# The last step of a decoder layer's output: part of y = x + rstd * out is scaled on ScalarE and added onto a copy of x by accumulating DMAs

## The reference

```
h = rmsnorm(x, g_pre);  proj = h @ w_in
yA = mLSTM branch of proj;  yB = gated-MLP branch of proj
merged = sigmoid(ga) * (yA @ w_pa) + sigmoid(gb) * (yB @ w_pb)
out = merged @ w_out
y = x + out * rsqrt(mean(out * out) + EPS) * g_post
```

## Time and profile before

| | us |
|---|---|
| median of 3 runs (lowest to highest) | 1534.61 (1534.37 to 1535.24) |
| the profiled execution, its own time | 1535.78 |
| its span, first to last instruction | 1534.3 |
| PE busy in the span | 1503.8 |
| from the last scalar rstd (L1619 begins at 1523.09) to the span's end | 11.2 |

### The profile page before, as it was taken

The page is one execution under the profiler, slowest core; times in us unless marked ns, Lnnn a source line. Parts: engine busy times, 40 slices in busy tenths (PEclk is TensorE's granted clock), DMA queues, the critical chain, the costliest instruction groups (busy, mean ns, idle before and its releaser), DMA issues.

```text
span 1534.3 us, 30736 instructions
## 1 busy us (share of the span) xinstructions
PE 1503.8 (98%) x11341; PEld 1497.0 (98%) x11341; DVE 892.8 (58%) x1526; ACT 658.3 (43%) x928; POOL 93.7 (6%) x171
## 2 busy tenths in 40 slices
PE   6999999999999999999999999999999999999996
PEld 6999999999999999999999999999999999999996
DVE  6756565654444457666766666666666644444444
ACT  6433433333333334454545454545444433333442
POOL 4000000001000000101010101001010000000000
PEclk9999999999999999999999999999999999999998
DMA  7664655556555554564738383747474555555553
GB/s 214 213 165 138 177 153 172 154 173 220 164 164 164 164 155 143 167 218 136 243 112 266 112 264 115 257 122 253 126 242 136 189 161 168 160 169 184 169 153 135
DMA packets 233905, 268.03 MB, mean 175 GB/s; under 512 B 9136, under 2 KB 222712, under 8 KB 232880
## 3 DMA queue, kind: packets, MB, share of 16 engines
q1 hardware_dynamic: 221472, 226.36, 49.3%
q0 software_dynamic: 12400, 41.23, 7.7%
HBM read 244.48 MB, written 23.06 MB: 174 GB/s over the span
## 4 chain that ended last, share of the span: by engine, by line
PE 92%; issue 6%; POOL 1%; DVE 1%; ACT 0%; DVEq 0%; POOLq 0%; ACTq 0%
PE ps L394 27%; PE ps L395 27%; PE ps L396 27%; PE ps L561 2%; PE ps L549 2%; PE ps L573 1%; PE ps L693 1%; PE ps L620 1%; PE ps L518 1%; DVE otok L1484 0%; PE ps L423 0%; PE ps L658 0%; PE ps L403 0%; PE ps L684 0%; PE ps L630 0%
## 5 line engine op out<-in xcount | busy, mean ns | idle before, releaser
L988 DVE TENSOR_TENSOR wlo<-raw,whi 128x1024 fp32r<-128x1024 f32 x416 | 507.9, 1224 | 558.0 <-ACT whi L745 556.3
L394 PE MATMUL ps<-xh,whi 128*128 128x288 f32 x2560 | 766.3, 299 | 0.0
L745 ACT ACTIVATE whi<-raw 128x1024 fp32r<-128x1024 f32 x416 | 440.5, 1059 | 746.1 <-PE ps L396 730.1
L396 PE MATMUL ps<-xh,wlo 128*128 128x288 f32 x2560 | 754.9, 295 | 0.0
L395 PE MATMUL ps<-xl,whi 128*128 128x288 f32 x2560 | 754.5, 295 | 0.0
L394 PEld LDWEIGHTS ps<-xh,whi 128*128 128x128 f32 x2560 | 481.1, 188 | 0.3
L395 PEld LDWEIGHTS ps<-xl,whi 128*128 128x128 f32 x2560 | 481.0, 188 | 0.2
L396 PEld LDWEIGHTS ps<-xh,wlo 128*128 128x128 f32 x2560 | 480.7, 188 | 0.0
L394 PE MATMUL ps<-yh,whi 128*128 128x288 f32 x512 | 151.6, 296 | 0.0
L395 PE MATMUL ps<-yl,whi 128*128 128x288 f32 x512 | 151.2, 295 | 0.0
L396 PE MATMUL ps<-yh,wlo 128*128 128x288 f32 x512 | 151.1, 295 | 0.0
(11 more groups left out here) (319 smaller groups left out, 1182.2 us busy)
## 6 DMA issues: line engine op xcount, KB each, us to landing
raw<-in_w_in_dram SPq DMA_DIRECT2D x320, 512.0 KB, 3.7
raw<-in_w_pb_dram SPq DMA_DIRECT2D x32, 512.0 KB, 3.5
Cin<-in_state_mlstm_C_dram POOLq DMA_DIRECT2D x16, 1024.0 KB, 8.7
out_dram<-Cin POOLq DMA_DIRECT2D x16, 1024.0 KB, 6.2
raw<-in_w_pa_dram SPq DMA_DIRECT2D x32, 512.0 KB, 3.5
raw<-in_w_out_dram SPq DMA_DIRECT2D x32, 512.0 KB, 3.6
xt<-in_x_prompt_dram SPq DMA_DIRECT2D x2, 1024.0 KB, 6.0
out_dram<-cpo POOLq DMA_DIRECT2D x8, 256.0 KB, 2.4
```

Source lines behind the costliest of these rows:

```text
L394: nc.tensor.matmul(out, whi[:, c, kk, cols], mh_[:, k, :], start=(k == 0), stop=False)
L396: last = nc.tensor.matmul(out, wlo[:, c, kk, cols], mh_[:, k, :], start=False, stop=(k == KT - 1))
L745: nc.scalar.activation(whi[:, c], raw[:, c], ACT.Copy).then_inc(hi_ready, 1)
L988: nc.vector.tensor_tensor(wlo[:, c], raw[:, c], whi[:, c].bitcast(F32), ALU.subtract).then_inc(lo_ready, 1)
```

## The change

Two of the six parts leave `Y_PARTS`: columns 1024 to 2047 of block 1 (128 x 1024) and block 2 (32 x 2048). For these, SP copies x straight from the input in DRAM to the output in DRAM (two DMAs, semaphore `y_base`), in its queue behind the load of `xres` and ahead of the stores; the load of the sample rows into `xres` is gone. ACT multiplies the two parts of `otok` by `rstd`, in place, once `o_rstd` and `otok_ev` are there (semaphore `y_scaled`). POOL, behind its power, waits for both copies and then for each part and issues a DMA from `otok` to the output that adds to what stands there (semaphore `y_sum`). It waits for both. DVE and SP keep the other four parts, in their order.

```
 Y_PARTS = ([(P, 0, slice(c, c + D // 4)) for c in (0, D // 4)] + [(P, 0, slice(D // 2, D))]
-           + [(P, 1, slice(c, c + D // 2)) for c in (0, D // 2)] + [(S, 2, slice(0, D))])
+           + [(P, 1, slice(0, D // 2))])
...
         sp.dma_start(xres[:, 0:2, :], xp_v).then_inc(x_again, 16)
-        sp.dma_start(xres[0:S, 2, :], xs_v).then_inc(x_again, 16)
-        y_rows = (y_prompt[0, 0:P, :], y_prompt[0, P:TP, :], y_sample.rearrange("b t d -> (b t) d"))
+        sp.dma_start(y_prompt[0, P:TP, HALVES[1]], x_prompt[0, P:TP, HALVES[1]]).then_inc(y_base, 16)
+        sp.dma_start(y_sample.rearrange("b t d -> (b t) d"), xs_v).then_inc(y_base, 16)
+        y_rows = (y_prompt[0, 0:P, :], y_prompt[0, P:TP, :])
...
         squares(1, 7)
+        act.wait_ge(o_rstd, 1)
+        act.wait_ge(otok_ev, 8)
+        for n, t, cols in ((P, 1, HALVES[1]), (S, 2, slice(0, D))):
+            nc.scalar.activation(otok[0:n, t, cols], otok[0:n, t, cols], ACT.Identity,
+                                 scale=rstd[0:n, t:t + 1]).then_inc(y_scaled, 1)
...
         dve.wait_ge(otok_ev, 8)
-        dve.wait_ge(x_again, 32)
+        dve.wait_ge(x_again, 16)
...
         nc.gpsimd.tensor_tensor(rstd[:], stat[:], half[:], ALU.pow).then_inc(o_rstd, 1)
+        pool.wait_ge(y_base, 32)
+        pool.wait_ge(y_scaled, 1)
+        pool.dma_start(y_prompt[0, P:TP, HALVES[1]], otok[:, 1, HALVES[1]], accum_op=ALU.add).then_inc(y_sum, 16)
+        pool.wait_ge(y_scaled, 2)
+        pool.dma_start(y_sample.rearrange("b t d -> (b t) d"), otok[0:S, 2, :], accum_op=ALU.add
+                       ).then_inc(y_sum, 16)
+        pool.wait_ge(y_sum, 32)
```

More of the change, by code:

```diff
@@ L298, in build @@
     cst_out, cp_out, nn_out, cs_out = sem("cst_out"), sem("cp_out"), sem("nn_out"), [sem("cs_out0"), sem("cs_out1")]
+    y_base, y_scaled, y_sum = sem("y_base"), sem("y_scaled"), sem("y_sum")
     x_again, g_post_in, o_sq, osq_set, o_var, o_rstd, y_set, y_out = (sem(n) for n in (
```

## The result

| | us |
|---|---|
| changed kernel, median of 11 runs (lowest to highest) | 1538.61 (1537.89 to 1539.25) |
| kernel before, timed beside it, median of 11 runs | 1535.24 (1533.97 to 1535.65) |
| ratio, 95% interval | 1.0023 (1.0016 to 1.0031) |
| changed kernel, profiled execution: its own time, its span | 1538.25, 1536.8 |

The kernel became 0.23% slower, 3.4 to 3.5 us. The time was inside the stated range (1533.0 to 1540.0), but not where the forecast stood (+0.6, with a band of its own from 0 to +1.5), and the ratio's interval lies on both sides of the 0.2% that was set as a bound. That the range held it owes much to luck: the range reached up to 1540.0 for rival A's sake, and rival A's mechanism is not what made the loss.

A forecast was written before the change was run, and what follows sets the result against it. PE bounds the kernel up to its last instruction, then DVE the tail by a thin margin; after the change, the DMA engines' work. Last data +0.55 and a second wait +0.05 give +0.6 on 1534.61: 1535.2 us, range 1533.0 to 1540.0.

The forecast's parts named there:

- rival A: In the tail, adds are served packet by packet, with gaps of 0.3 to 0.95 us: +0.75 to +7.2 us; chance 0.3.
- DVE, SP, ACT: In the tail, DVE loses two parts, SP's last store is issued near 1527.8, ACT's scalings take 1.14 and 2.0 us.
- POOL's issues: In the tail, POOL's adds are issued near 1525.75 and 1527.7, each issue taking 0.62 us.
- The copies hidden: Ahead of the tail, the DRAM-to-DRAM copies cost nothing, being there by about 1508, 17 us ahead of use.
- Last data of before at 1532.95: In the tail, last data of the kernel before were put at 1532.95, against 1533.5 after the change: +0.55 us.
- An add is twice a store: On the tail's DMA engines, each added byte costs a store and a load: 2 x 1.95 = 3.9 us.
- 3.9 us for the adds: In the tail, the DMA engines' work for 0.75 MB of adds, on top of 3.9 us for four stores: 7.85 us.
- The sample rows at 2.6 us per MB: In the tail, the 0.25 MB sample rows were priced at the stores' 2.6 us per MB, one more read at 0.65 us.
- No idle time until the last data: In the tail, DMA engines work without a gap from 1525.66 to 1533.5, the first add filling the hole at 1527.
- 0.05 us for POOL's wait at the end: At the kernel's end, a second wait adds +0.05 us to the sum.
- Rival B: In the tail, an add costs no more than a store: -1.4 us, 1533.2; chance 0.17.
- Rival C: In the tail, POOL's queue brings its own bandwidth and adds run beside SP's stores: -3.3 us, 1531.3; chance 0.03.

The follow-up runs named there:

- the marks: Changed kernel with two 128 x 1 fills on POOL, one behind its wait for the adds, one behind its old waits; one execution, tail 15.1 us.

## Why the prediction was right or wrong, point by point

- *Everything ahead of the tail stays:* right. The tail alone holds the 3.6 us; its start moved by 1.1 us the other way, within what kernels that are alike up to there show.
- *DVE, SP, ACT:* right. DVE stopped after 3.8 us, ACT's two scalings took 1.15 and 1.99 us (1.14 and 2.0 foretold), SP's last store went out 4.74 us into the tail, as before.
- *POOL's issues:* a little off, and it cost nothing. With the add they took 0.94 and 0.82 us, the plain ones in the same place 0.61 and 0.53; the first was issued 1.73 us behind ACT's start where the sum had 1.75, the second 3.34 where it had 3.7.
- *The copies hidden:* right, and with more room than was claimed: all is quiet from about 1504, not 1508.
- *Last data of before at 1532.95:* misread. That is where the last packet starts; it ends at 1533.50. By its own work the sum (1533.5) gives +0.0 for the last data and not +0.55.
- *An add is twice a store:* right for an ordinary packet of 4 KB, 0.33 us against 0.16. The Trainium skill's factor of two, from "Collectives: The Full Stack", section on why ReduceScatter is half of AllGather, which gives 1.93 as measured there, agrees with these packets, whose source is in on-chip memory. It does not fit the sample rows, 0.63 us added against 0.62 stored; there the measurement decides.
- *3.9 us for the adds:* 5.0 were measured, and this is the term of the sum that was mis-sized. The ordinary packets alone come to what was priced: on each engine eight of 0.328 us and two of 0.628 make 3.9. The other 1.1 us are packets that took longer, and the sum had no term for them. Most are at the start of an add: the first 16 of the changed kernel took 0.86 us each (0.48 to 1.43), where an ordinary one takes 0.33.
- *The sample rows at 2.6 us per MB:* wrong, and it did little harm in the adds' price, because two errors nearly cancel there. Stored from 32 partitions they cost about 1.2 us of the engines' time before (shares 1.86 and 1.53), twice their price by bytes, 0.65. Yet as an add they cost 1.4 to 1.5 us, where twice 0.65 was foretold. The length of their packets alone isn't the reason: `xres`, loaded in packets of 8 KB too, came at 426 GB/s.
- *No idle time until the last data:* nearly. 9.05 us of work (5.0 + 4.0) took 9.75 us from the first data to the end of the last, most of the idle time being in the last microsecond, in which the engines don't finish together. With +1.2 us of work and this 0.7 the last data end 1.9 us later in the tail.
- *0.05 us for POOL's wait at the end:* wrong, and the one step that missed a mechanism: 1.7 us more than before from the last data to the end, 1.6 when taken alone. I counted what is queued behind POOL's adds, the old waits, but took the end of a queue to be free. The profile of before could not show the price, as POOL had left long before SP did. No rival had it either.
- *Rival A,* packet by packet with gaps of 0.3 to 0.95 us: its time (+0.75 to +7.2) holds the result, and that is luck, since its mechanism is seen only at the start of an add. Both bounds of its gap came from the misreading above. An ordinary added packet of 4 KB takes 0.33 us, two plain ones 0.32, so between those there is no gap of 0.3 us.
- *Rival B,* an add at a store's price: refuted for the 128 x 1024 part, 3.5 us against 1.3, and true for the sample rows. Even so it would not have gained the 1.4 us that I gave it: with plain stores and the end taken away the tail is 0.1 us shorter, because of the sample rows' price (1.4 us instead of 0.65) and the last data of before, which I had 0.55 us too early.
- *Rival C,* the queues side by side: refuted. SP's two later stores landed after 6.6 and 7.9 us instead of 2.8, because they shared the engines with the adds. The section "Issuing engines are not separate DMA queues" of the Trainium skill's page "DMA: Bandwidth & Descriptors" agrees with this.

## What to carry to other kernels

A tail is bound by the sum of the DMA engines' work as soon as the compute chain ends near the last data. Moving arithmetic into the DMA then makes the bound longer, here by 2.2 us for the 128 x 1024 part (3.5 instead of 1.3) and by nearly nothing for the sample rows. Price a transfer by the packets' time that its own stretch shows (share times length), not by its bytes, and do so above all for stores from few partitions; and remember that a packet counts where it starts, so that a share above 1 followed by an empty stretch is an engine at work and not a burst and a gap. Last, look at who waits last: an engine whose way out is slow (here POOL's, 2.9 us) should end early, and the final wait should stand on one whose way out is short (SP's, 0.4 to 0.7 us).

## What the runs showed of the hardware that I had not expected

- From POOL's last wait to the span's end 2.9 us pass (1533.93 to 1536.8 behind the marks, 1533.3 to 1536.2 in the kernel before with one more wait). From SP's last landing it is 0.4 us before (1533.9 to 1534.3) and 0.7 us where SP waits for the adds (1535.1 to 1535.8). Why POOL's is longer the runs do not say.
- An accumulating DMA from on-chip memory to DRAM takes 1.9 times the engines' time of the same plain stores, alone as well as beside stores. By parts it is 2.7 times for rows of 4 KB in 128 partitions and about the same time for rows of 8 KB in 32 partitions. The issue takes some 0.3 us more of POOL's time.
- The first packet that each engine serves of the first add takes 0.5 to 2.4 us; with the sample add alone nothing else started on any engine for 1.0 us meanwhile.
- A DVE instruction with two inputs in on-chip memory took 5.51 us instead of 1.27 beside a POOL sum of 4.8 us.
